# Attention jobs of a two-layer decoder, two to a TensorE visit instead of one

## What is computed

```
h = rmsnorm(x)
q_a, k_a, v_a, q_b, k_b, v_b, z, xbc, dt = split(h @ w_in)
# A: window of 128 keys, causal, sink in the denominator, RoPE on q and k
s = q_a k_a^T * 64**-0.5 (masked);  m = max(s, sink);  p = exp(s - m)
y_a = (p / (sum(p) + exp(sink - m))) v_a
# B: causal softmax over all 256 keys
y_b = softmax(q_b k_b^T * 64**-0.5 (masked)) v_b
y_c = ssd(z, xbc, dt)
x += (g_a * (y_a @ w_br_a) + g_b * (y_b @ w_br_b) + g_c * (y_c @ w_br_c)) @ w_mix_out
x += cross_attention(...) @ w_co;   x += square(relu(rmsnorm(x) @ w_up)) @ w_down
```

## Time and profile before

| | us |
|---|---|
| median of 3 runs (1178.24 to 1179.38) | 1179.04 |
| the profiled execution | 1178.97 |
| its span | 1177.2 |
| PE busy | 1166.1 |
| DVE busy | 775.1 |
| ACT busy | 596.3 |

### The profile page before, as it was taken

One profiled execution on the slowest core, in us unless ns is written; L12 is line 12 of the kernel. 1 busy time (PEld: TensorE's weight loads), 2 busy tenths in 40 slices (PEclk: granted clock), 3 DMA queues, 4 the chain that ended last, 5 costly groups with the idle time before them and its releaser, 6 DMA issues.

```text
span 1177.2 us, 18388 instructions
## 1 busy us (share of the span) xinstructions
PE 1166.1 (99%) x7491; PEld 1036.0 (88%) x7491; DVE 775.1 (66%) x1199; ACT 596.3 (51%) x870; POOL 61.1 (5%) x93
## 2 busy tenths in 40 slices
PE   8999999999999999999999999999999999999997
PEld 7988899999998888888889888999989988888886
DVE  7876856987455475665578677579775455766565
ACT  5656564445454354444455666453555444544443
POOL 1000003300000000000000000033000000000000
PEclk9999999999999999999999999999999999999999
DMA  7744426765644456556456443455755443755660
GB/s 238 237 143 132 156 85 187 220 213 176 194 143 151 136 180 204 188 180 199 159 156 205 144 144 108 140 172 191 250 179 180 144 143 111 244 182 180 202 208 37
DMA packets 156428, 201.31 MB, mean 171 GB/s; under 512 B 7168, under 2 KB 111928, under 8 KB 156344
## 3 DMA queue, kind: packets, MB, share of 16 engines
q1 hardware_dynamic: 155616, 199.58, 53.2%
q10 hardware_dynamic: 728, 0.55, 0.1%
HBM read 199.04 MB, written 1.08 MB: 170 GB/s over the span
## 4 chain that ended last, share of the span: by engine, by line
PE 94%; DMA 2%; DVE 1%; issue 1%; ACT 1%; POOL 1%; SPq 0%; POOLq 0%; DVEq 0%; ACTq 0%
PE psum L1153 12%; PE psum L1154 12%; PE psum L1155 12%; PE psum L1164 11%; PE psum L1165 10%; PE psum L1139 10%; PE psum L1167 10%; PE psum L1140 5%; PE psum L1186 1%; PE psum L1318 1%; PE psum L1356 1%; DMA raw<-in_w_gate_dram 1%; PE psum L1329 1%; PE psum L1374 1%; PE psum L1397 1%
## 5 line engine op out<-in xcount | busy, mean ns | idle before, releaser
L1499 DVE TENSOR_TENSOR w_lo<-raw,w_hi 128x2048 fp32r<-128x2048 f32 (+1 forms) x182 | 408.9, 2251 | 221.3 <-ACT w_hi L755 220.7
L755 ACT ACTIVATE w_hi<-raw 128x2048 fp32r<-128x2048 f32 (+1 forms) x182 | 341.6, 1879 | 158.2 <-PE psum L1167 109.6
L1153 PE MATMUL psum<-act_both,w_hi 128*128 128x256 f32 x832 | 241.0, 290 | 0.0
L1154 PE MATMUL psum<-act_both,w_hi 128*128 128x256 f32 x832 | 235.2, 283 | 0.0
L1155 PE MATMUL psum<-act_both,w_lo 128*128 128x256 f32 x832 | 235.2, 283 | 0.0
L1139 PE MATMUL psum<-act_both,w_hi 128*128 128x512 f32 x512 | 182.1, 400 | 0.0
L1153 PEld LDWEIGHTS psum<-act_both,w_hi 128*128 128x128 f32 x832 | 159.2, 191 | 4.1 <-issue 3.0
L1154 PEld LDWEIGHTS psum<-act_both,w_hi 128*128 128x128 f32 x832 | 159.3, 192 | 0.6 <-issue 0.5
L1155 PEld LDWEIGHTS psum<-act_both,w_lo 128*128 128x128 f32 x832 | 159.2, 191 | 0.0
L1140 PE MATMUL psum<-act_both,w_lo 128*128 128x256 f32 x512 | 143.7, 281 | 0.0
L1139 PEld LDWEIGHTS psum<-act_both,w_hi 128*128 128x128 f32 x512 | 96.2, 188 | 24.6 <-DVE act_both L1528 0.7
(11 more groups left out here) (261 smaller groups left out, 1928.2 us busy)
## 6 DMA issues: line engine op xcount, KB each, us to landing
raw<-in_w_in_dram SPq DMA_DIRECT2D x34, 1024.0 KB, 5.2
raw<-in_w_up_dram SPq DMA_DIRECT2D x32, 1024.0 KB, 5.4
raw<-in_w_down_dram SPq DMA_DIRECT2D x32, 1024.0 KB, 5.0
raw<-in_w_gate_dram SPq DMA_DIRECT2D x24, 1024.0 KB, 7.3
raw<-in_w_ckv_dram SPq DMA_DIRECT2D x16, 1024.0 KB, 5.3
raw<-in_w_br_ssd_dram SPq DMA_DIRECT2D x8, 1024.0 KB, 5.4
raw<-in_w_mix_out_dram SPq DMA_DIRECT2D x8, 1024.0 KB, 5.0
raw<-in_w_cq_dram SPq DMA_DIRECT2D x8, 1024.0 KB, 5.2
```

What stands on the lines that cost most here:

```text
L755: act.activation(w_hi[:, slot, 0:n], raw[:, slot, 0:n], ACT.Copy).then_inc(hi_ready.sem, 1)
L1153: pe.matmul(dst, m_hi[:, k, cs], a_hi[:, k, :], start=k == 0, stop=False)
L1154: pe.matmul(dst, m_hi[:, k, cs], a_lo[:, k, :], start=False, stop=False)
L1499: dve.tensor_tensor(w_lo[:, slot, 0:n], raw[:, slot, 0:n], w_hi[:, slot, 0:n].bitcast(F32), ALU.subtract).then_inc(lo_ready.sem, 1)
```

## The change

Jobs 2k and 2k + 1 make a couple (`COUPLES` holds the even ones up to 14). In the slot of an even job PE computes the scores of both jobs of the couple, in one visit; the two share banks 4 and 5, each job in half the columns of both (`score_cols`), and one semaphore count, given by the odd job's matmuls, tells that both are there. Both jobs' mask passes wait for that one count. The bank is given free by the odd job's pass; the even one marks its own two steps and settles them before it goes on. The values of both jobs stand three slots after the even one's scores, which is an odd job's slot. Turns stay one to a visit, one slot behind the job's own slot. So a visit in an even job's slot has the scores of two jobs and one turn, and a visit in an odd job's slot has one turn and the values of two jobs.

No scores stand ahead of the turn any more, and the values of jobs 0 and 1 follow it. The diff:

```diff
--- before.py
+++ after.py
@@ -185,6 +185,14 @@
 S_HEAD = SEQ + 4
 
 
+COUPLES = range(0, SSD_JOB0, 2)
+
+
+def score_cols(n):
+
+    return slice((n % 2) * SEQ, (n % 2) * SEQ + (job_of(n)[1] + 1) * P)
+
+
 def head_of(j, i):
 
 
@@ -232,11 +240,13 @@
             out.append((YB_, ("closeT", i)))
     if s == SWA_T_SLOT:
         out += [(b, ("qkT", i)) for i, b in enumerate((SB_, TB_, OB_))]
-    if 0 <= job_at(s) < SSD_JOB0:
+    if job_at(s) in COUPLES:
         out += [(SB_, ("score", job_at(s), 0)), (TB_, ("score", job_at(s), 1))]
     if 0 <= job_at(s - 1) < SSD_JOB0:
         out.append((YB_, ("probsT", job_at(s - 1))))
-    if job_at(s - 2) in [0, 4, 8, 12, 16, 18, 20, 22]:
+    if job_at(s - 3) in (0, 4, 8, 12):
+        out.append((OB_, ("values", job_at(s - 3))))
+    if job_at(s - 2) in (16, 18, 20, 22):
         out.append((OB_, ("values", job_at(s - 2))))
     if s == STATES_SLOT:
         out += [(YB_, ("states", 0)), (SB_, ("states", 1))]
@@ -1308,15 +1318,17 @@
                     wait_read(pe, l, [("qkT", i) for i in range(1, 3)])
                 if n == 8:
                     wait_read(pe, l, [(first_of("qkb", i), 0) for i in range(4)] + [unit_bank(U_VB, t) for t in range(TT)])
-                for i in range(2):
+                for i in range(2) if n in COUPLES else ():
                     pe.wait_ge(*is_free(l, ("score", n, i)))
                 qk = (qkT_a, qkT_b)[branch]
                 k_tile = 4 + (j // 2 if branch == 0 else j)
                 for i in range(2):
-                    key = ("score", n, i)
+                    key = ("score", n - n % 2, i)
                     half_p = slice(i * HD, (i + 1) * HD)
-                    pe.matmul(bank(key)[:, 0:(t + 1) * P], qk[half_p, j, t * P:(t + 1) * P],
-                              qk[half_p, k_tile, 0:(t + 1) * P], start=True, stop=True).then_inc(full(key), 1)
+                    ins = pe.matmul(bank(key)[:, score_cols(n)], qk[half_p, j, t * P:(t + 1) * P],
+                                    qk[half_p, k_tile, 0:(t + 1) * P], start=True, stop=True)
+                    if n not in COUPLES:
+                        ins.then_inc(full(key), 1)
 
             def job_turn(l, n):
                 branch, t, j = job_of(n)
@@ -1424,8 +1436,9 @@
                     h = u - CROSS_SLOT0
                     if u == SWA_T_SLOT:
                         swa_turn(l)
-                    if 0 <= job_at(u) < SSD_JOB0:
-                        job_scores(l, job_at(u))
+                    if job_at(u) in COUPLES:
+                        for n in (job_at(u), job_at(u) + 1):
+                            job_scores(l, n)
                     if 0 <= job_at(u - 1) < SSD_JOB0:
                         job_turn(l, job_at(u - 1))
                     for i, (_, branch, c, g) in enumerate(CLOSINGS):
@@ -1436,7 +1449,10 @@
                             pe.wait_ge(*is_free(l, key))
                             pe.matmul(bank(key), xbcT[:, 10 + g, P:2 * P], states[:, g, :],
                                       start=True, stop=True).then_inc(full(key), 1)
-                    if 0 <= job_at(u - 2):
+                    if job_at(u - 3) in COUPLES:
+                        for n in (job_at(u - 3), job_at(u - 3) + 1):
+                            job_values(l, n)
+                    if job_at(u - 2) >= SSD_JOB0:
                         job_values(l, job_at(u - 2))
                     if u == STATES_SLOT:
                         pe.wait_ge(*xdec_ready.at(l, 1))
@@ -1805,7 +1821,7 @@
                 branch, t, j = job_of(n)
                 if n < SSD_JOB0:
                     for i in range(2):
-                        dve.wait_ge(*is_full(l, ("score", n, i)))
+                        dve.wait_ge(*is_full(l, ("score", n - n % 2, i)))
                 else:
                     dve.wait_ge(*acs_spread.at(l, 16 * (n - SSD_JOB0 + 1)))
                 if 2 <= n < 18:
@@ -1831,11 +1847,16 @@
                     sinks = s_sb[:, n % 2, :].rearrange("p (i k) -> p i k", k=S_HEAD)[:, :, keys:keys + 1]
                     steps.mark(dve.tensor_copy(sinks, cols[:, l, c:c + 2].unsqueeze(2)))
                 for i in range(2):
-                    c, key = i * S_HEAD, ("score", n, i)
-                    dve.tensor_tensor_reduce(s_sb[:, n % 2, c:c + keys], bank(key)[:, 0:keys], mask, 1.0,
-                                             -3.0e38, ALU.add, ALU.max, row_max[:, i:i + 1]).then_inc(free(key), 1)
-                for i in range(2):
-                    dve.wait_ge(*is_read(l, ("score", n, i)))
+                    c, key = i * S_HEAD, ("score", n - n % 2, i)
+                    ins = dve.tensor_tensor_reduce(s_sb[:, n % 2, c:c + keys], bank(key)[:, score_cols(n)], mask, 1.0,
+                                                   -3.0e38, ALU.add, ALU.max, row_max[:, i:i + 1])
+                    if n in COUPLES:
+                        steps.mark(ins)
+                    else:
+                        ins.then_inc(free(key), 1)
+                steps.settle()
+                for i in range(2) if n not in COUPLES else ():
+                    dve.wait_ge(*is_read(l, ("score", n - 1, i)))
                 if branch == 0:
                     c = PC_SINK + head_of(j, 0)
                     steps.link(dve.tensor_tensor(row_max[:], row_max[:], cols[:, l, c:c + 2], ALU.max))
```

## The result

The change took **1183.80 us** (median of six runs, 1183.36 to 1183.93) against 1178.86 for the kernel before (six runs, 1178.24 to 1179.38). The ratio is 1.0041, interval 1.0029 to 1.0054. The forecast was 1172.5 and faster; the kernel is slower by 4.9 us and lies 7 us above the top of the range.

What follows compares the result with a forecast made beforehand. PE bounds the kernel: its own instructions plus holes between its groups. Measured 1179.04 less 11.4 of saved edges plus 4.9 of new waiting gave 1172.5 us, with a range of 1167.8 to 1176.6.

Steps and rivals of the forecast that it cites:

- What bounds the kernel: Time is PE's own instructions plus holes between its groups; a full visit pays 0.71 us of edges, none round transposes.
- Parts 1 and 2: Coupling scores, and values one visit later, on PE saves 0.71 us per couple, 11.4 us in two layers; joins cost zero.
- B: Rival: each of 32 joins on PE shows a weight load of 0.107 us, +3.4, giving 1175.9 us; chance 0.10.
- Part 3: Semaphores, settles and DVE's mask passes: changed waits and earlier masks cost or gain PE zero.
- Part 5: Even jobs' turns on PE newly wait for scaled probabilities (jobs 2, 4, 14, and 6): 4.9 us given back.
- A: Rival: ACT and DVE chains run ahead, so the new waits before turns vanish: 1167.6 us, half gone 1170; chance 0.17.
- C: Rival: odd visits hold ACT for values, unabsorbed by idle time: 1175.5 to 1185 us; chance 0.12, half slower than 1181.4.
- D: Rival: PE's holes belong to waits before groups, so only score edges go, some 3 us, 1176; chance 0.06.
- Part 2: Values of two jobs joined in one PE visit, one visit later, saving the 0.35 us value edges in every other visit.
- Part 4: In odd visits ACT's copy of turned probabilities is held some 0.37 us for values; its idle absorbs it, so zero.

Runs made afterwards that it cites:

- sp_after: The changed kernel with SP's weight loads of units 27 and 28 moved ahead of the small loads for jobs 16 and 17; 1172.49 us.
- early2: sp_after plus exponentials (ACT) and reciprocals (DVE) of jobs 2, 4 and 14 alone moved ahead of the weight split; 1167.78 us.
- early: sp_after plus exponentials (ACT) and reciprocals (DVE) of jobs 2, 4, 6, 8 and 14 moved ahead of the weight split; 1173.95 us.
- before_held: The kernel before the change, with SP waiting for the values of job 15 instead of job 14 before the load for job 16; 1188.77 us.

## Why the prediction was wrong

- **What bounds the kernel** was right: time is PE's own work and the holes round the groups. Edges stand round the groups of 64 rows and of 64 columns, and not round the transposes.
- **Parts 1 and 2, the edges**: right in kind and size. 11.4 us were forecast. `sp_after` saves 6.3 us with 4.8 of waits in it, so the edges gave about 11.1; `early2`, with the waits gone, saves 10.8, and its trace gains 5.58 by unit 25 of the first layer (forecast 5.68). The joins cost nothing, so B is false: its 3.4 us would show in both, and eight score records took 0.22 more than four.
- **Part 3, semaphores and DVE**: no sign of a cost in any slot.
- **Part 5, the new wait**: right. 4.9 us forecast, 4.8 read as idle time of the weight loads. Job by job, as the visit's length in the change less that in `early2`, which has no wait there: job 2 0.36 (forecast 0.38), job 4 0.84 (0.84), job 14 1.03 (1.07), 4.5 in both layers. Job 6 of the second layer, forecast at 0.36, isn't in the list. (With job 6 of the first layer at 0.1 the prediction's own terms add up to 5.0, not 4.9.) A, which had the waits vanish, is false for the change as it stands, and C's growing hold isn't seen either. D is false by `sp_after`.
- **Part 2, who waits for the moved values: the step that failed.** It costed the values of job 14 as work of PE that stands one slot later, and never asked what else counts on them. Part 4 asked it of ACT and stopped there. The wait of SP for `values_done` is no line that the change touches, and it stands in the stream of weights. "Outside the job slots nothing should move" is the sentence that the profile refutes: SP's small load moved by 3.7 us, the weight tile of unit 27 with it, and 11.3 us were lost, nearly all at units 27 to 31 of the two layers. The range, drawn from rivals that all lay inside the job slots, had no case for it. C was slower as well, but for another reason, and its slower half had 6 in 100.
- **The size of that step** could in part have been seen ahead, from the rows of the kernel before. The tile left SP at 167.90 and ACT took it up at 175.06, 7.2 us later, without waiting for it. In the changed kernel 8.0 us lie between 171.64 and 179.68, and ACT waited for the whole of it. So ACT had no slack to speak of: 3.7 us for the issue and 0.9 for the longer load make the 4.6 by which ACT and DVE were late. PE had some. The bank was taken 0.84 us after the merge began where PE waited for it (185.47 to 186.31), and 6.8 us after it before the change (180.87 to 187.68): 6.0 us of slack. A merge 4.6 later and a PE 3.2 earlier are 7.8, which is 1.8 too much; the first matmul of unit 27 was 1.9 late. DVE's last write of `y_tok` and PE's first matmul on it in the kernel before:

```profile
205.80 0.49 DVE L1880 TENSOR_SCALAR y_tok<-y_tok,srstd 128x512 f32<-128x512 f32 x1 [0.94 <-POOL srstd L726]
...
207.95 0.61 PE L1365 MATMUL psum<-ident,y_tok 128*128 128x128 f32 x4
```

In the change this write starts at 208.10, 2.3 later, and PE's matmul at 208.64, 0.54 behind it; before, 2.15 lay between, so the slack was 1.6. With PE 1.7 ahead by then, 2.3 + 1.7 - 1.6 = 2.4 had to be waited, and were.

What stays open is why the losses differ between kernels with the same hold (11.3 us in the change, 9.6 with the values alone, 10.0 without couples). The clock falls in both layers of the change and in the second layer alone of the other two. A fall cost 1.3 and 1.5 in the two places where it is worked out above, but the layers of the kernel without couples speak against it as the reason, and no run took the clock alone away.

## What to carry to other kernels

Before a step is moved one slot later, look up every wait on the count that it raises, on all engines, and on the queue that issues the DMAs first: what stands *behind* such a wait pays, however small the load that waits is. Work out the slack at that place, and not only that of the weight tile itself (issue, landing, first use): here the tile had 8.4 us to spare on PE and kept 2.4 of them, and the loss came from what ACT and DVE do behind it, which had 6.0 and 1.6. A kernel that gains on TensorE also asks for those results earlier. And when two savings make one engine faster, the waits they uncover are found one by one: give an engine's early work only to the jobs that wait, since each move ahead puts something else behind.

## What the runs showed of the hardware

The granted clock can fall behind a short wait. It fell to its lower level behind a stretch of 2 us in which PE was busy 0.92, and projection matmuls then started 0.21 apart for 1.7 us instead of 0.12. In `early` it fell behind a wait of 1.9 us. It did not fall everywhere: in the first layer of `before_held` PE was busy 0.84 of the 2 us from 210 on and the clock read 1.00 there and behind; and in layer 1 of the change PE was busy 0.84 of 3 us and the clock read 1.00 in that stretch and in the next (the columns are those of the windows above):

```profile
767.00:770.00 3.00, 0.84 (x5) 0.56 (x5) 3.00 (x9) 2.34 (x4) 0.47 (x1) 1.00 0.06 5
770.00:773.00 3.00, 3.00 (x27) 3.00 (x26) 3.00 (x2) 0.36 (x1) 0.85 (x1) 1.00 0.93 176
```

A wait may then cost more than its length, and this one is not to be foretold from its length alone. The mean clock of the run, 0.997 where the kernel before has 0.999, hardly shows it. The waits before the turns, up to 1.0 us, never did it: the clock reads 1.00 from 47 to 175 us.
